# A stacked fp32r product for the samples' new states in a state-space scan, and another order of the steps around it

## What is computed

```python
proj = rmsnorm(x) @ w_in                      # -> z, xBC, dt, glu
x, B, C = silu(conv4(xBC))                    # 32 heads of 64, 4 groups of B and C, state 128
# chunked scan, for each head; h0 is the state that a sample brings along
y   = (C B^T * decay * dt) x  +  exp(cum) * C h0
h_n = exp(cum_last) * h0  +  B^T (decay_to_end * dt * x)      # the new state, an output
g   = group_rmsnorm((y + d_skip * x) * silu(z))
mix = concat(g, conformer(glu)) @ w_out
```

## Time and profile before

| | |
|---|---|
| median of 3 runs | 1793.79 us (1793.65 to 1793.89) |
| the profiled execution's own time | 1794.34 us |
| its span | 1792.7 us |
| PE busy | 1775.9 us, 99% |
| DVE busy | 1089.4 us, 61% |
| ACT busy | 763.9 us, 43% |
| POOL busy | 449.3 us, 25% |
| granted clock of PE | 0.999 |
| chain that ended last | PE 96%, DVE 2%, ACT 1% |

### The profile page before, as it was taken

How to read it: one execution, slowest core, us unless ns; L and a number is a source line. 1 busy time by engine, 2 the same in 40 slices (tenths; PEclk the granted TensorE clock), 3 DMA queues, 4 the chain that set the end, 5 groups by cost and what they waited for, 6 DMA issues and landing times.

```text
span 1792.7 us, 34869 instructions
## 1 busy us (share of the span) xinstructions
PE 1775.9 (99%) x13199; PEld 1742.6 (97%) x13199; DVE 1089.4 (61%) x2004; ACT 763.9 (43%) x1116; POOL 449.3 (25%) x351
## 2 busy tenths in 40 slices
PE   8999999999999999999999999999999999999998
PEld 7999999999998989999899999999999999999998
DVE  5587878999778777865875333444344444444444
ACT  7443435555356565633543333333333332333442
POOL 1577776677651222223000000000000000000132
PEclk9999999999999999999999999999999999999999
DMA  8555554554545555554345444544444444454442
GB/s 253 190 177 159 154 155 134 153 153 143 156 150 167 161 181 161 190 192 141 118 145 161 141 152 146 161 152 141 151 138 160 155 147 142 140 158 155 155 142 83
DMA packets 287305, 278.42 MB, mean 155 GB/s; under 512 B 11590, under 2 KB 284718, under 8 KB 286336
## 3 DMA queue, kind: packets, MB, share of 16 engines
q1 hardware_dynamic: 249064, 247.87, 44.0%
q10 hardware_dynamic: 36496, 21.77, 4.1%
q0 software_dynamic: 1648, 7.43, 1.3%
HBM read 261.25 MB, written 17.22 MB: 155 GB/s over the span
## 4 chain that ended last, share of the span: by engine, by line
PE 96%; DVE 2%; ACT 1%; DMA 0%; issue 0%; SPq 0%; DVEq 0%; ACTq 0%
PE ps L1801 29%; PE ps L1803 29%; PE ps L1802 29%; PE ps L2095 1%; PE ps L2045 1%; PE ps L2068 1%; PE ps L2105 1%; PE ps L2139 1%; PE ps L1859 1%; PE ps L2141 1%; PE ps L2140 1%; PE ps L1860 1%; PE ps L1861 1%; DMA xn<-in_x_prompt 0%; DVE mix L1668 0%; DVE wlo L1198 0%
## 5 line engine op out<-in xcount | busy, mean ns | idle before, releaser
L1801 PE MATMUL ps<-ahi,whi 128*128 128x320 f32 x2304 | 717.9, 312 | 0.0
L1803 PE MATMUL ps<-ahi,wlo 128*128 128x320 f32 x2304 | 711.9, 309 | 0.0
L1802 PE MATMUL ps<-alo,whi 128*128 128x320 f32 x2304 | 711.9, 309 | 0.0
L681 ACT ACTIVATE whi<-raw 128x1024 fp32r<-128x1024 f32 x463 | 478.4, 1055 | 446.7 <-PE ps L1803 383.0
L1198 DVE TENSOR_TENSOR wlo<-raw,whi 128x1024 fp32r<-128x1024 f32 x344 | 424.3, 1257 | 236.6 <-ACT whi L681 233.7
L1801 PEld LDWEIGHTS ps<-ahi,whi 128*128 128x128 f32 x2304 | 432.5, 188 | 2.1 <-issue 0.5
L1802 PEld LDWEIGHTS ps<-alo,whi 128*128 128x128 f32 x2304 | 432.6, 188 | 0.5
L1803 PEld LDWEIGHTS ps<-ahi,wlo 128*128 128x128 f32 x2304 | 432.5, 188 | 0.0
L1801 PE MATMUL ps<-hhi,whi 128*128 128x320 f32 x1016 | 314.3, 309 | 0.0
L1803 PE MATMUL ps<-hhi,wlo 128*128 128x320 f32 x1016 | 313.9, 309 | 0.0
L1802 PE MATMUL ps<-hlo,whi 128*128 128x320 f32 x1016 | 313.9, 309 | 0.0
(11 more groups left out here) (324 smaller groups left out, 1603.6 us busy)
## 6 DMA issues: line engine op xcount, KB each, us to landing
raw<-in_w_in SPq DMA_DIRECT2D x144, 512.0 KB, 3.5
raw<-in_w_up SPq DMA_DIRECT2D x128, 512.0 KB, 4.2
raw<-in_w_down SPq DMA_DIRECT2D x128, 512.0 KB, 4.5
raw<-in_w_out SPq DMA_DIRECT2D x64, 512.0 KB, 3.7
h<-in_state_ssm ACTq DMA_DIRECT2D x16, 512.0 KB, 4.9
out<-hout ACTq DMA_DIRECT2D x16, 512.0 KB, 3.2
x_transposed<-xt ACTq DMA_DIRECT2D x1, 2560.0 KB, 13.5
xr<-x_transposed POOLq DMA_DIRECT2D x1, 2560.0 KB, 9.6
```

Source lines behind the costliest of these rows:

```text
L681: act.activation(whi[:, kq, :, 0:width], raw[:, kq, :, 0:width], ACT.Copy).then_inc(hi_done, 1)
L1801: pe.matmul(out, wh, hi[:, kk, :], start=(kk == 0), stop=False)
L1802: pe.matmul(out, wh, lo[:, kk, :], start=False, stop=False)
L1803: last = pe.matmul(out, wl, hi[:, kk, :], start=False, stop=(kk == NT - 1))
```

## The change

The change sets up, for i of 1 to 3, one product over all 128 rows in fp32r in place of the plain float32 product over 32 rows. B and the weighted x are each split into a high part (fp32r) and the rest. The stationary tile `xq[h]` holds x high in rows 64 to 127, x high of the own half in rows 32 to 63 and x low in rows 0 to 31; the moving tile `bq` holds masked B high, masked B low and masked B high in the same places. The product over the 128 rows is the sum of the three. For i = 0 the old product stays.

What builds them: PE transposes the samples' part of the next group's B at j = 1 (into free columns of bank 3); ACT copies it out (`b_rows`), makes eight masked copies at j = 2 (`b_masked`), eight of the low part at j = 3 (`b_low`) and two wider ones (`b_high`); DVE makes the low part of B at j = 2 (`b_lowest`). In each step with i >= 1 ACT makes two copies of `xdd` directly behind the first Exp and two more behind `h0t`, and DVE two subtractions directly behind the first weighted product (1541).

What else moves: ACT's `ahead(2j + 1)` goes from the middle of the step to its top, behind `ahead(2j)`; the second distances go ahead of `hts` and `ecb`, and `hts` ahead of `ecb`, with the Exp behind them; DVE's `pst` goes ahead of the new states `hout`; on PE the 32 small matmuls go from behind the prompt's last state to directly behind the new states; `bm` is made only for i = 0. Semaphores that nothing used are removed.

```diff
@@ -151,7 +151,12 @@
         mix = place("mix", [P, NT, TOK], at=ar)
         sc = ar + 5120
         btok = place("btok", [P, 3, P], at=sc + 640)
-        bm = place("bm", [P, NB, P], at=sc + 1024)
+        bts = place("bts", [P, P], at=sc)
+        bthi = place("bthi", [P, P], F32R, at=sc + 128)
+        btlo = place("btlo", [P, P], at=sc + 256)
+        xq = [place("xq0", [P, P], F32R, at=sc + 384), place("xq1", [P, P], F32R, at=sc + 512)]
+        bm = place("bm", [P, NB, P], at=ar + 12 * TOK)
+        bq = [place("bq0", [P, NB, P], F32R, at=ar + 12 * TOK), place("bq1", [P, NB, P], F32R, at=sc + 1024)]
         xd = place("xd", [P, 3, P], at=sc + 2048)
         xdd = place("xdd", [P, 3, P], at=sc + 2432)
         h0t = place("h0t", [P, NB, P], at=sc + 2816)
@@ -961,6 +968,31 @@
             conf_silu(2)
 
 
+            def b_rows(transposed):
+                act.activation(bts[64:P, :], transposed, ACT.Copy)
+                act.activation(bthi[64:P, :], transposed, ACT.Copy).then_inc(bts_ready, 1)
+
+            def b_masked(i):
+                act.wait_ge(bts_ready, i)
+                for b in range(NB):
+                    last = act.activation(bq[i % 2][64:P, b, :], bts[64:P, :], ACT.Copy, scale=blk[64:P, b:b + 1])
+                last.then_inc(bq_ready, 1)
+
+            def b_low(i):
+                act.wait_ge(btlo_done, i)
+                for b in range(NB):
+                    own = slice(64 + 32 * (b // 4), 96 + 32 * (b // 4))
+                    last = act.activation(bq[i % 2][32:64, b, :], btlo[own, :], ACT.Copy, scale=blk[own, b:b + 1])
+                last.then_inc(bq_ready, 1)
+
+            def b_high(i):
+                act.wait_ge(bq_ready, 3 * i - 2)
+                for h in range(2):
+                    own = slice(64 + 32 * h, 96 + 32 * h)
+                    last = act.activation(bq[i % 2][0:32, 4 * h:4 * h + 4, :],
+                                          bq[i % 2][own, 4 * h:4 * h + 4, :].bitcast(F32), ACT.Copy)
+                last.then_inc(bq_ready, 1)
+
             def load_h0(T, slot):
                 act.dma_start(h0[:, slot], state_ssm[0].rearrange("b (t e) p n -> (e p) t b n", e=2)[:, T]
                               ).then_inc(h0_in[slot], 16)
@@ -974,13 +1006,15 @@
                 act.dma_start(p_ssm[0, 0].rearrange("(t e) p n -> (e p) t n", e=2)[:, T], pst[:]
                               ).then_inc(pst_out, 16)
 
-            def decay(T, e):
+            def distances(T, e):
                 act.wait_ge(seg_done, 2 * T + e + 1)
                 for c in range(3):
                     lo, hi = c * P, min((c + 1) * P, TOK)
                     last = act.activation(wgt[:, e, lo:hi], ps[:, 3, lo:hi], ACT.Relu, scale=-1.0,
                                           bias=tcol[:, c, ds(2 * T + e, 1)])
                 last.then_inc(span_done, 1)
+
+            def decays(T, e):
                 act.wait_ge(span_done, 2 * T + e + 1)
                 act.activation(wgt[:, e, :], wgt[:, e, :], ACT.Exp, scale=-1.0).then_inc(exp_done, 1)
 
@@ -1004,6 +1038,8 @@
                     T = 4 * i + j
                     first = isinstance(i, int) and i == 0 and j == 0
                     ahead(Q_WC, i, 2 * j)
+                    if not first:
+                        ahead(Q_WC, i, 2 * j + 1)
                     if j == 0:
                         act.wait_ge(bt_trans, i + 1)
                         act.activation(btok[:], ps[:, 4, 0:384].rearrange("p (c n) -> p c n", c=3), ACT.Copy
@@ -1012,11 +1048,22 @@
                         conf_silu(3)
                     else:
                         act.wait_ge(y_done, T)
-                    decay(T, 0)
+                    distances(T, 0)
+                    decays(T, 0)
+                    if i:
+                        act.wait_ge(xd_ready, T + 1)
+                        act.wait_ge(st_done, T)
+                        for h in range(2):
+                            act.activation(xq[h][64:P, :], xdd[64:P, 2, :], ACT.Copy).then_inc(xhi_done, 1)
                     act.wait_ge(h0_trans, T + 1)
                     act.activation(h0t[:, 0:4, :], ps[:, 6, :].rearrange("p (b n) -> p b n", b=4), ACT.Copy)
                     act.activation(h0t[:, 4:8, :], ps[:, 7, :].rearrange("p (b n) -> p b n", b=4), ACT.Copy
                                    ).then_inc(h0t_ready, 1)
+                    if i:
+                        act.wait_ge(xhi_done, 2 * T - 6)
+                        for h in range(2):
+                            last = act.activation(xq[h][32:64, :], xdd[64 + 32 * h:96 + 32 * h, 2, :], ACT.Copy)
+                        last.then_inc(xq_ready, 1)
                     if not first:
                         act.wait_ge(hnew_done, T)
                     if not (final and j == 3):
@@ -1025,14 +1072,19 @@
                         gate_hi(i - 2)
                     if j == 1 and i >= 1:
                         gate_keep(i - 1)
-                    ahead(Q_WC, i, 2 * j + 1)
+                    if first:
+                        ahead(Q_WC, i, 2 * j + 1)
+                    distances(T, 1)
+                    act.wait_ge(pstart_done, T + 1)
+                    act.activation(hts[:], ps[:, 4, 384:512], ACT.Copy).then_inc(hts_ready, 1)
                     act.wait_ge(ecb_mm, T + 1)
                     if not first:
                         act.wait_ge(y_read, T)
                     act.activation(ecb[:], ps[:, 2, TOK:512], ACT.Copy).then_inc(ecb_ready, 1)
-                    act.wait_ge(pstart_done, T + 1)
-                    act.activation(hts[:], ps[:, 4, 384:512], ACT.Copy).then_inc(hts_ready, 1)
-                    decay(T, 1)
+                    decays(T, 1)
+                    if j == 1 and i < 3:
+                        act.wait_ge(bts_trans, i + 1)
+                        b_rows(ps[64:P, 3, TOK:448])
                     if j % 2:
                         p = j // 2
                         act.wait_ge(weights_used, 4 * (Q_WC + 2 * i + p) + 4)
@@ -1040,6 +1092,11 @@
                                        ).then_inc(read_act, 1)
                     if j == 1 and i >= 1:
                         gate_root(i - 1)
+                    if j == 2 and i < 3:
+                        b_masked(i + 1)
+                    if j == 3 and i < 3:
+                        b_low(i + 1)
+                        b_high(i + 1)
                     store_h(T)
 
             act.wait_ge(dt_ready, 1)
@@ -1515,6 +1572,11 @@
                                              in1=ghi[:, t, :].bitcast(F32), op0=ALU.mult, op1=ALU.subtract
                                              ).then_inc(gact_ready, 1)
 
+            def b_lowest(i):
+                dve.wait_ge(bts_ready, i)
+                dve.tensor_tensor(btlo[64:P, :], bts[64:P, :], bthi[64:P, :].bitcast(F32), ALU.subtract
+                                  ).then_inc(btlo_done, 1)
+
             def wc(i):
                 for j in range(4):
                     T = 4 * i + j
@@ -1539,10 +1601,17 @@
                         conf_act(2)
                     dve.wait_ge(exp_done, 2 * T + 1)
                     dve.tensor_tensor(wgt[:, 0, :], cb, wgt[:, 0, :], ALU.mult).then_inc(mixw_done, 1)
-                    if j == 0:
+                    if i:
+                        dve.wait_ge(xhi_done, 2 * T - 6)
+                        for h in range(2):
+                            own = slice(64 + 32 * h, 96 + 32 * h)
+                            last = dve.tensor_tensor(xq[h][0:32, :], xdd[own, 2, :], xq[h][own, :].bitcast(F32),
+                                                     ALU.subtract)
+                        last.then_inc(xq_ready, 1)
+                    if j == 2 and i < 3:
+                        b_lowest(i + 1)
+                    if first:
                         dve.wait_ge(btok_ready, i + 1)
-                        if not first:
-                            dve.wait_ge(st_done, 4 * i)
                         dve.tensor_tensor(bm[:], btok[:, 2, :].unsqueeze(1).to_broadcast([P, NB, P]),
                                           blk[:].unsqueeze(2).to_broadcast([P, NB, P]), ALU.mult
                                           ).then_inc(bm_ready, 1)
@@ -1564,15 +1633,15 @@
                     if not first:
                         dve.wait_ge(hout_out, 16 * T)
                         dve.wait_ge(pst_out, 16 * T)
+                    v = st.inc(dve.tensor_scalar(s0s[:], ps[:, 4, 0:P], ecb[:, P - 1:P], None, ALU.mult))
+                    dve.wait_ge(dve_step, v)
+                    dve.tensor_tensor(pst[:], ps[:, 4, P:2 * P], s0s[:], ALU.add).then_inc(pst_done, 1)
                     for b in range(NB):
                         col = P + DS * b + DS - 1
                         last = dve.scalar_tensor_tensor(
                             out=hout[:, b, :], in0=h0[:, j % 2, b, :], scalar=ecb[:, col:col + 1],
                             in1=ps[:, 6 + b // 4, (b % 4) * P:(b % 4 + 1) * P], op0=ALU.mult, op1=ALU.add)
```

(34 more changed lines are left out.)

14 lines of the change are left out of this document (8 added, 6 removed).

## The result

The changed kernel takes 1800.24 us (median of 7 runs, 1798.8 to 1800.7), the kernel before, beside it on the same chip, 1793.93 us (7 runs, 1793.65 to 1794.4): ratio 1.0033, 95% interval 1.0023 to 1.0043. It is 6.3 us slower. The forecast was 1794.2, with a range up to 1798.0; both are missed, on the slow side. The profiled execution after took 1800.37 us (span 1798.8).

What follows compares the result with a forecast made beforehand. PE bounds the kernel, busy 1775.9 of 1792.7 us. Terms -6.0 + 0.35 - 0.5 + 2.6 + 4.0 = +0.45 us on the profiled 1794.34; with the median 0.55 below, forecast 1794.2 us, range 1787.0 to 1798.0.

Steps and rivals of the forecast that it cites:

- The saving: New pair for the samples' states on PE: 0.56 us instead of 1.06, 0.50 less in 12 steps, -6.0 us.
- The transposes: One added on PE at j = 1 for i = 0 to 2: 3 x 0.12 = +0.35 us, up to 0.75.
- Step 1: PE's 1.4 us wait for `pst` goes, but transposes of the old states need `hnew_done`: -0.5 us (0 to -1.4).
- ACT's top of the step: ACT's first split of a step starts 1.06 us later, at t0 + 3.12, a second split of 0.95 behind it.
- j = 0: PE waits 0.9 us for `btok` in steps 4, 8 and 12: +2.6 us (0.7 to 1.1 each).
- They cost nothing again: Distances, Exp and `h0t`, queued behind `btok` on ACT at j = 0, cost nothing: PE is a granule away.
- Rival 2: Slower: `pst` issue on ACT takes 1.62 us, not 0.42; PE stands 1.2 longer per hit; 1797.8 us, chance 0.19.
- j = 2: PE waits for the second weighted product, 1.4 us in steps 6 and 10, 1.2 in step 14: +4.0 us.
- The chain of the second product: DVE's work up to that product at j = 2, without gaps, ends 1.35 us later, at 634.46.
- DVE's new operations: Two subtractions and, for i < 3, `b_lowest` on DVE at j = 2: 0.2 us each, 0.6 in all.
- j = 1 and 3: Steps without a table load: no new wait of PE, counted 0, up to 0.1 us each if not (+1.2).
- ordinary issue: Both store issues on ACT now follow the last DVE write: 0.4 us more ahead of a step's first split.

Runs made afterwards that it cites:

- the filled gap: Changed kernel with 7, 14 and 7 dummy matmuls on PE while it waits for `btok` at steps 4, 8 and 12: 1800.5 us.
- the store on GpSimd: Changed kernel with the store of `pst` issued by GpSimd instead of ACT: 1794.44 us, ratio to the kernel before 1.0002.
- the order alone: Kernel before with only the moves of the change, the old plain float32 pair kept: 1799.11 us, ratio 1.0028.
- the GpSimd runs: Store of `pst` issued by GpSimd instead of ACT: changed kernel 1794.44 us, kernel before with only the change's moves 1794.58, kernel before 1794.04.

## Why the prediction was wrong

- **The saving.** The mechanism was right, the size was not. The pair costs 0.18 us more than two matmuls of the earlier trace rows, where 0.10 was counted for the change of type, so by itself it saves 0.42 and not 0.50. But it also starts 0.17 sooner behind the middle state, which the prediction did not look at. Together this is 0.59 a step, 7.1 us where 6.0 was counted, in the bounds of 4.8 to 7.2. The forecast did not fail by this term: it was too careful by 1.1 us.
- **The transposes.** +0.35 predicted; one took 0.11 us. Right.
- **Step 1.** -0.5 predicted and 0.1 for the transpose, +0.1 measured for both. The transposes do wait for `hout` instead, 0.84 us, and another 0.28 for the first weighted product follows. That wait was a third one in a row, and I had stopped at the second.
- **ACT's top of the step.** Predicted at t0 + 3.12, measured t0 + 3.29. Right. The two issues back to back cost what I said and 0.17 more: the second one takes 0.59 us behind the first, where it took 0.42 alone.
- **j = 0.** The wait of 0.9 is there in steps 4 and 12 (1.00 and 0.99). "They cost nothing again" was the step that failed. The prediction named the distances, the Exp and `h0t` as what is queued behind `btok` on ACT. It left out the four copies of x high that the change itself puts there (0.51 and 0.63 us), in steps 8 and 12 the four copies of `gate_hi` (1.92), and `hts` behind all of them. Step 12 is 1.35 us longer instead of 0.37: PE waits 0.61 for `hts` and 0.17 for the second product, 0.9 together by the starts. The lateness of `btok` isn't the cause of that. Between `btok` and the distances ACT stands idle for 0.84 us, until PE's segment, and the wait for `hts` is 0.60 to 0.62 behind waits for `btok` of 0.59, 0.86, 0.99 and 1.27 (the filled gap, the store on GpSimd, the changed kernel). It is the length of ACT's list from there to `hts`. It takes the copies and `gate_hi` together: step 4 without `gate_hi` and the order alone without the copies have no such wait.
- **Rival 2, the long issue.** It came once in this trace, at step 8. The prediction priced a hit at 1.2 us and said that it decides from three hits of six. The hit makes step 8 16.68 long, 1.87 more than step 12: the 1.2 of the issue, and the rest because the clock fell behind the gap. I had not asked what PE does after a gap.
- **j = 2.** The chain of the second product was right in its form. Predicted +2.5, measured +3.7: another 0.4 us a step. In steps 6 and 10 the product ends 0.40 later than predicted (634.86, not 634.46), and the term that was mis-sized is that of DVE's new operations. The new subtractions put 1.05 us between the first product and the reciprocal on DVE (631.23 - 629.77, less the 629.34 - 628.93 of the earlier trace rows), not 0.6. And I never asked when the new pair's own last operand, `xq` on ACT, would be there: 1.22 us of PE's wait stand ahead of it. In steps 6 and 10 this wait adds nothing, since PE would stand for DVE's product until the same moment. In step 14, which has no `b_lowest`, it is the only one, and the step is 13.35 long instead of 13.03.
- **j = 1 and 3.** -1.3 and -1.5 predicted, -1.3 and -1.1 measured. The agreement at j = 1 is partly luck: a saving of 0.59 and not 0.50 a step, less 0.16 in steps 5 and 9, in which ACT's queue holds the pair. At j = 3 it holds it for 0.19 to 0.29, where the prediction counted 0 to 0.1.

By size: of the 5.9 us between forecast and result in these sums, j = 0 has 3.9 (the long issue with the clock 1.9, the late `hts` and what follows it 1.0 in step 12 and, counted by step 12, 1.0 in step 8), j = 2 1.2, step 1 0.5, j = 3 0.4, less the 0.2 by which step 1 starts earlier. Without the long issue the changed kernel would stand near 1800.2 - 1.9 = 1798.3, an estimate from the length of step 12, and still be slower than before. Rival 2 therefore had the right culprit, the store issue with no cover, as the GpSimd runs show, and the wrong weight: it counted only the long issues, while the ordinary issue, 0.6 us in each of steps 4, 6, 10 and 14 and 0.5 in step 1, is worth more than the one long issue. Of that ordinary issue the forecast itself had counted 0.4.

## What to carry to other kernels

An instruction that waits in an in-order queue, above all a DMA issue, is free only where the engine would stand idle anyway; when steps are moved to the top of a queue, price what every later entry of that queue feeds, up to the end of the step, and the operand of the new instruction first of all. When a saving comes back as waits, take the short cheap instructions off the engine whose queue is full before moving its large ones, and look whether the engine that takes them slows its neighbour. A gap on PE costs more than its length once the clock falls, but that price can lie under another wait: filling the gap gained nothing here with the next wait still in place. A wait also has to be read from the starts of the instructions around it: a list that begins at modelled ends left out up to 0.3 us of each here.
